# Decay exponents of the state-space block as one fp32r product with a block-diagonal matrix kept in DRAM

## The reference, cut to what matters

```python
def _ssd(xs, dt, a, bm, cm):            # 2 chunks of L = 128 tokens, 32 heads
    a_dt = (dt * a)...                   # [chunk, head, 128]
    a_cs = jnp.cumsum(a_dt, axis=-1)
    seg = a_cs[..., :, None] - a_cs[..., None, :]
    decay_in = jnp.exp(jnp.where(tril, seg, -jnp.inf))
    cb = jnp.einsum('bclgn,bcsgn->bgcls', Cc, Bc)
    y_diag = jnp.einsum('bgecls,bcsgep->bclgep', cb[:, :, None] * decay_in, X)
    ...
```

## Time and profile before

| | |
|---|---|
| median of 3 runs | 2217.0 us (2216.79 to 2220.03) |
| profiled execution | 2215.97 us, span 2214.2 us |
| granted TensorE clock | 0.995 of full speed over the span |
| TensorE busy | 2175.9 us, 98% of the span |
| VectorE, ScalarE, GpSimd busy | 1422.0, 999.5, 102.6 us |
| DMA | 409.23 MB, mean 185 GB/s |

### The profile page before, as it was taken

One profiled execution on the slowest core, in us unless ns is written; L12 is line 12 of the kernel. 1 busy time (PEld: TensorE's weight loads), 2 busy tenths in 40 slices (PEclk: granted clock), 3 DMA queues, 4 the chain that ended last, 5 costly groups with the idle time before them and its releaser, 6 DMA issues.

```text
span 2214.2 us, 29921 instructions
## 1 busy us (share of the span) xinstructions
PE 2175.9 (98%) x11250; PEld 1794.6 (81%) x11250; DVE 1422.0 (64%) x2126; ACT 999.5 (45%) x1486; POOL 102.6 (5%) x122
## 2 busy tenths in 40 slices
PE   6999999999999999999999999999999999999999
PEld 1587888897778888888778888888888888888887
DVE  2267665646846676787788545687778787644455
ACT  3243242434544444555466445544444444344453
POOL 1020100102010120000000000000000000000000
PEclk8999999999999999999999999999999999999999
DMA  9976565543045666665413565666666666655674
GB/s 372 384 227 209 200 209 187 164 122 97 10 167 177 211 200 190 180 184 174 148 39 94 181 190 185 211 191 183 192 180 189 187 189 190 200 190 190 190 244 164
DMA packets 209908, 409.23 MB, mean 185 GB/s; under 512 B 15501, under 2 KB 24069, under 8 KB 208264
## 3 DMA queue, kind: packets, MB, share of 16 engines
q1 hardware_dynamic: 205536, 386.71, 55.7%
q0 software_dynamic: 3360, 16.76, 2.6%
q10 hardware_dynamic: 904, 4.29, 0.5%
HBM read 400.49 MB, written 7.22 MB: 184 GB/s over the span
## 4 chain that ended last, share of the span: by engine, by line
PE 90%; DVE 4%; DMA 3%; ACT 1%; issue 1%; POOL 0%; SPq 0%; DVEq 0%; ACTq 0%
PE bank L2085 52%; PE bank L2095 19%; PE bank L2099 10%; DMA ada_ring<-in_w_ada 2%; PE bank L2211 1%; PE bank L2321 1%; PE bank L2269 1%; PE bank L2308 1%; DVE wlo L1283 1%; PE bank L2235 1%; PE bank L2220 1%; DMA raw<-in_w_in 1%; PE bank L2499 0%; DVE st L1489 0%; PE bank L2391 0%
## 5 line engine op out<-in xcount | busy, mean ns | idle before, releaser
L2085 PE MATMUL bank<-whi,xhl 128*128 128x512 f32 (+2 forms) x3776 | 1136.7, 383 | 3.4 <-DVE wlo L1283 3.0
L1283 DVE TENSOR_TENSOR wlo<-raw,whi 128x1024 fp32r<-128x1024 f32 (+2 forms) x649 | 773.2, 1204 | 463.7 <-ACT whi L773 442.4
L773 ACT ACTIVATE whi<-raw 128x1024 fp32r<-128x1024 f32 (+2 forms) x649 | 664.1, 1047 | 667.1 <-PE bank L2085 344.6
L2085 PEld LDWEIGHTS bank<-whi,xhl 128*128 128x128 f32 x3776 | 695.5, 188 | 140.1 <-DVE wlo L1283 6.5
L2085 PE MATMUL bank<-wlo,xhl 128*128 128x512 f32 (+2 forms) x1888 | 719.9, 381 | 0.0
L2095 PE MATMUL bank<-xhl,whi 128*128 128x512 f32 x1792 | 489.4, 394 | 0.0
L2085 PEld LDWEIGHTS bank<-wlo,xhl 128*128 128x128 f32 x1888 | 354.4, 188 | 67.4
L2095 PEld LDWEIGHTS bank<-xhl,whi 128*128 128x128 f32 x1792 | 306.3, 189 | 41.5 <-issue 0.3
L2099 PEld LDWEIGHTS bank<-xhl,wlo 128*128 128x128 f32 x1792 | 275.0, 189 | 38.2
L2099 PE MATMUL bank<-xhl,wlo 128*128 128x256 f32 x1792 | 285.0, 281 | 0.0
L1946 DVE TENSOR_TENSOR up_x<-bank,up_x 128x256 f32<-128x256 f32 x88 | 31.2, 417 | 72.2 <-ACT up_x L780 72.2
(11 more groups left out here) (361 smaller groups left out, 1383.8 us busy)
## 6 DMA issues: line engine op xcount, KB each, us to landing
raw<-in_w_in SPq DMA_DIRECT2D x216, 512.0 KB, 4.1
raw<-in_w_up SPq DMA_DIRECT2D x176, 512.0 KB, 3.7
raw<-in_w_out SPq DMA_DIRECT2D x96, 512.0 KB, 4.6
raw<-in_w_down SPq DMA_DIRECT2D x88, 512.0 KB, 4.7
ada_ring<-in_w_ada SPq DMA_DIRECT2D x64, 512.0 KB, 11.4
gate_w<-in_w_ada SPq DMA_DIRECT2D x32, 512.0 KB, 3.9
raw<-in_w_ple_gate SPq DMA_DIRECT2D x32, 512.0 KB, 4.8
raw<-in_w_in SPq DMA_DIRECT2D x16, 384.0 KB, 3.8
```

The costliest lines, as they stand in the source:

```text
L773: nc.scalar.activation(whi[:, slot, 0:size], raw[:, slot, 0:size], ACT.Copy).then_inc(hi_ready, 1)
L1283: tt_(wlo[:, slot, 0:size], raw[:, slot, 0:size], whi[:, slot, 0:size].bitcast(F32), ALU.subtract).then_inc(lo_ready, 1)
L2085: ins = mm(b4[tt][:, 0:width], x[:, o:o + P], w, start=k == 0 and i == 0, stop=k == last and i == 2)
```

## The change

It builds the exponents another way. The cumulative sums themselves are computed by TensorE with heads on partitions (one 128x128 product for each chunk, from a copy of a_dt that stands four times side by side, the last two times negated), and are split into a high and a low fp32r part (`CH`, `CL`).

- A DRAM tensor `m_dram` of 2 x 128 x 4096 floats holds, for each head, a block of 128 columns. It is first filled from the constants, which grow by 4096 columns (two copies from DRAM to DRAM of 2 MB each, on GpSimd's queue, right behind the load of `h` and ahead of the constants). Later four DMAs write the positive high and low sums on its block diagonal, rows 0 to 63. Rows 64 to 127 keep ones in each head's block.
- `STA`, the stationary operand of a chunk, has ones in rows 0 to 63 and the negated high and low sums in rows 64 to 127. One fp32r product of `STA` with 512 columns of `m_dram` then gives sum at l minus sum at s for four heads.
- The mask is added in the same bank by an fp32r product of the identity with the mask (0 or -1e30), read four times.
- `RR` is no longer computed: GpSimd loads 256 KB of `m_dram` into it for each batch, so `seg_rows` is gone from VectorE and ScalarE.
- In the loop over b the batches of `seg` are now issued in pairs, behind the products of odd b.

```diff
...
+K_DIAG = 1610
+K_W = K_DIAG + 4096
...
+    c[:, K_SLT:K_SLT + P] = np.where(i[:, None] <= i[None, :], 0, NEG)
+    for h in range(32):
+        c[64 + h::32, K_DIAG + P * h:K_DIAG + P * (h + 1)] = 1.0
...
+        m_dram = nc.dram_tensor("cumsum_diag_dram", (NT, P, 4096), F32).ap()
...
             g.dma_start(H[:, :, :], a["x"][0].rearrange("(t p) n -> p t n", p=P)).then_inc(s_h, 16)
+            for t in range(NT):
+                g.dma_start(m_dram[t], a["const"][:, K_DIAG:K_DIAG + 4096]).then_inc(s_mz, 16)
             g.dma_start(KC2[:, :], a["const"][:, K_SWA:K_SWA + 5 * P]).then_inc(s_t5, 16)
...
+            g.wait_ge(s_mz, 32)
+            g.wait_ge(s_clo, 1)
+            for t in range(NT):
+                for rows, part in ((0, CH), (32, CL)):
+                    corner = m_dram[t, rows:rows + 1, 0:1]
+                    diag = bass.AP(corner.tensor, corner.offset, [[4096 + P, 32], [1, P]])
+                    g.dma_start(diag, part[rows:rows + 32, t, :].bitcast(F32)).then_inc(s_md, 16)
+            g.wait_ge(s_md, 64)
+            g.wait_ge(xb_ready, 6)
+            for b in range(16):
+                if b == 2:
+                    g.wait_ge(xd_ready, 1)
+                if b >= 4:
+                    g.wait_ge(seg_ps, b - 3)
+                g.dma_start(RR[b % 4][:, :, :].rearrange("p h l -> p (h l)").bitcast(F32),
+                            m_dram[b // 8, :, W * (b % 8):W * (b % 8 + 1)]).then_inc(seg_in[b % 4], 16)
...
+                if i == 4:
+                    act.wait_ge(s_cst, 1)
+                    copy(CH[:, :, :], bank[3][:, 0:2 * P].rearrange("p (t l) -> p t l", t=NT)).then_inc(s_chi, 1)
+                if i == 7:
+                    act.wait_ge(s_clo, 1)
+                    copy(STA[0:64, 0, :], KC2[0:64, 512:640])
+                    own(copy(STA[0:64, 1, :], KC2[0:64, 512:640]))
+                    copy(STA[64:96, :, :], CH[64:96, :, :].bitcast(F32))
+                    copy(STA[96:128, :, :], CL[96:128, :, :].bitcast(F32))
+                    copy(MSKR[:, :], KC2[:, 384:512])
+                    copy(IDR2[:, :], ID[:, :]).then_inc(s_sta, 1)
...
+                    for t in range(NT):
+                        for k in range(4):
+                            ins = ts_(ADT4[:, t, 32 * k:32 * k + 32], ADT[:, t, :], 1.0 - 2.0 * (k // 2), None, ALU.mult)
+                    ins.then_inc(s_adt4, 1)
...
+                if i == 5:
+                    dve.wait_ge(s_chi, 1)
+                    tt_(CL[:, :, :], bank[3][:, 0:2 * P].rearrange("p (t l) -> p t l", t=NT),
+                        CH[:, :, :].bitcast(F32), ALU.subtract).then_inc(s_clo, 1)
...
-                tt_(RR[b % 4][:, :, :], tri3, b32(ADT[:, t, h0:h0 + 4], P), ALU.mult).then_inc(seg_in, 1)
...
             def seg(b):
...
+                pe.wait_ge(seg_in[b % 4], 16 * (b // 4 + 1))
                 if b >= 4:
                     pe.wait_ge(seg_e, b - 3)
-                mm(bank[b % 4][:, :], SLT, RR[b % 4][:, :, :].rearrange("p h l -> p (h l)"), start=True,
+                mm(bank[b % 4][:, :].rearrange("p (h l) -> p h l", h=4), IDR2[:, :],
+                   MSKR[:, :].rearrange("p (h l) -> p h l", h=1).to_broadcast([P, 4, P]), start=True, stop=False)
+                mm(bank[b % 4][:, :], STA[:, b // 8, :], RR[b % 4][:, :, :].rearrange("p h l -> p (h l)"), start=False,
                    stop=True).then_inc(seg_ps, 1)
...
+                    pe.wait_ge(s_adt4, 1)
+                    for t in range(NT):
+                        ins = mm(bank[3][:, P * t:P + P * t], ADT4[:, t, :], TRI, start=True, stop=True)
+                    ins.then_inc(s_cst, 1)
...
-                if b + 4 < 16:
+                if b % 2 and b < 13:
+                    seg(b + 3)
                     seg(b + 4)
...
```

More of the change, by code:

```diff
@@ L194, in build @@
         MR = [at(f"m_ring{i}", o, [P, 4, P]) for i, o in enumerate((51032, 51544, 8192))]
-        RR = [at(f"r_ring{i}", o, [P, 4, P]) for i, o in enumerate((47104, 47616, 43008, 43520))]
+        RR = [at(f"r_ring{i}", o, [P, 4, P], FR) for i, o in enumerate((47104, 47616, 43008, 43520))]
+        ADT4, STA = at("adt_signed", 50656, [P, NT, P]), at("cumsum_stationary", 50656, [P, NT, P], FR)
+        CH, CL = at("cumsum_high", 51032, [P, NT, P], FR), at("cumsum_low", 51288, [P, NT, P], FR)
+        MSKR, IDR2 = at("decay_mask_r", 50384, [P, P], FR), at("ident_r2", 50512, [P, P], FR)
         BT = at("b_t", 48128, [P, 4, P])
@@ L297, in build @@
         yo_ps, yo_done = sem("y_off_psum"), sem("y_off_added")
-        seg_in_a = sem("seg_in_by_scalar")
-        seg_in, seg_ps, seg_e, m_ready = sem("seg_in"), sem("seg_psum"), sem("seg_exp"), sem("m_ready")
+        seg_in = [sem(f"seg_rows_loaded{i}") for i in range(4)]
+        seg_ps, seg_e, m_ready = sem("seg_psum"), sem("seg_exp"), sem("m_ready")
+        s_adt4, s_cst, s_chi, s_clo, s_sta = (sem("adt_signed"), sem("cumsum_rows_psum"), sem("cumsum_high"),
+                                              sem("cumsum_low"), sem("cumsum_stationary"))
+        s_mz, s_md = sem("cumsum_diag_zeros"), sem("cumsum_diag_stored")
         y_mm, y_out = sem("y_products"), sem("y_added")
@@ L1123, in _ @@
             act.wait_ge(qk_ready, 1)
[L1124 to L1131, removed]
             for b in range(16):
@@ L1713, in dt_part @@
                     own(stt(DT, DT_V, 0.0, DT_L, ALU.max, ALU.add))
-                    stt(ADT, DT, -1.0, DT_EA.rearrange("p (a h) -> p a h", a=1).to_broadcast([P, NT, 32]),
-                        ALU.mult, ALU.mult).then_inc(s_dt_v, 1)
+                    own(stt(ADT, DT, -1.0, DT_EA.rearrange("p (a h) -> p a h", a=1).to_broadcast([P, NT, 32]),
+                            ALU.mult, ALU.mult))
+                    dve.sem_inc(s_dt_v, 1)
+                    for t in range(NT):
+                        for k in range(4):
+                            ins = ts_(ADT4[:, t, 32 * k:32 * k + 32], ADT[:, t, :], 1.0 - 2.0 * (k // 2), None, ALU.mult)
+                    ins.then_inc(s_adt4, 1)
                     own(ts_(NSINK, S2[:, 96:128], -1.0, None, ALU.mult))
@@ L1874, in _ @@
                 tt_(m_ring(b), m_ring(b), over_heads(CBT[:, t, g4, :], 4), ALU.mult).then_inc(m_ready, 1)
-                if b + 4 < 16 and b + 4 not in SEG_BY_ACT:
-                    seg_rows(b + 4)
                 if b == 3:
@@ L2380, in _ @@
             jobs(N_O1, J_O1, O1_T, 256, moving=R_O1)
-            TRI, SLT, ONE = KC2[:, 256:384], KC2[:, 384:512], KC2[:, 512:640]
+            TRI, ONE = KC2[:, 256:384], KC2[:, 512:640]
             def seg(b):
[L2384 to L2388, removed]
+                pe.wait_ge(seg_in[b % 4], 16 * (b // 4 + 1))
                 if b >= 4:
                     pe.wait_ge(seg_e, b - 3)
-                mm(bank[b % 4][:, :], SLT, RR[b % 4][:, :, :].rearrange("p h l -> p (h l)"), start=True,
+                mm(bank[b % 4][:, :].rearrange("p (h l) -> p h l", h=4), IDR2[:, :],
+                   MSKR[:, :].rearrange("p (h l) -> p h l", h=1).to_broadcast([P, 4, P]), start=True, stop=False)
+                mm(bank[b % 4][:, :], STA[:, b // 8, :], RR[b % 4][:, :, :].rearrange("p h l -> p (h l)"), start=False,
                    stop=True).then_inc(seg_ps, 1)
```

16 lines of the change are left out of this document (2 added, 14 removed).

## The result

| | before | changed |
|---|---|---|
| median | 2217.01 us (6 runs, 2216.78 to 2220.03) | 2225.97 us (6 runs, 2225.2 to 2228.47) |
| profiled execution | 2215.97 us, span 2214.2 | 2226.18 us, span 2224.4 |
| granted TensorE clock over the span | 0.995 | 0.992 |

The ratio is 1.004, with a 95% interval of 1.0029 to 1.005: the change costs 9.0 us. The forecast was 2225.8 us.

What follows compares the result with a forecast made beforehand. TensorE, busy 98% of the span, was taken as the bound. Profiled execution 2215.97 - 5.6 (loop) + 14.4 (fill) = 2224.8 us; the median, 1.0 us above, gives 2225.8 us; 8-in-10 range 2212 to 2234.

Steps and rivals of the forecast that it cites:

- The fill's loss: Start of the first output projection: the fill of m_dram starves the weight stream, TensorE loses 14.4 us; chance 0.52.
- the length of the fill: Two DRAM-to-DRAM copies behind the load of h: 22.1 us, with reading and writing sharing 403 GB/s.
- the margin: Near 650 us: VectorE has tiles A and B ready 3.5 and 3.6 us before TensorE comes to them.
- The loop's side: Loop of decays, 1093 to 1134 us: 6.2 us less, 0.6 us added on TensorE, so 5.6 us gained.
- Packets one to one: During the fill, DMA engines alternate queues packet by packet whatever the size; weights get about 256 packets of 2 KB, 0.52 MB.
- The case of no starving: Rival at the fill: the weight queue gets what it asks for, TensorE never waits; 2211.4 us, chance 0.19.
- the third case: The fill hardly hurts the weights, for instance if engines drain many descriptors per turn; 2211.4 us, chance 0.19.
- the short case: At the fill: each byte counts once at 403 GB/s, so it lasts 11.7 us and the loss is 4.0 us.
- The small copies "at nothing": Eight small copies and one subtraction on VectorE (some 1.5 us), ScalarE's copies (some 2 us): no cost, covered by ScalarE's waits.
- the lower bound of 3 us: Loop of decays: gain of only 3 us if VectorE and ScalarE hold the pace from batch 5 on.
- that rival: Loop of decays: RR loads need 12 us and come late, 13.5 us on top, 2239 us; chance 0.03.
- The rival of a short fill: At the fill: a byte counts once, over in 11.7 us, loss 4.0 us; 2215.4 us, chance 0.26.

Runs made afterwards that it cites:

- e7: The kernel before with TensorE's part alone: exponents' product in fp32r, seg_rows kept, no fill, cumulative sums or loads; 2219.56 us against 2217.65, ratio 1.0008.

## Why the prediction was right, and where it was not

The time came out within 0.2 us of the forecast. That is closer than the steps deserve, and the closeness is luck. The fill's loss was to be 14.4 us and was 13.7, but the length of the fill and the margin behind this sum were each wrong by several microseconds, in opposite directions. The loop's side was to be -5.6 us and was -3.4 (-4.7 + 0.9 + 0.45). For the profiled execution the sum gave 2224.8 us and 2226.18 came; the 1.0 us added for the median, which lay 0.2 us below that execution this time, made up for it.

**Packets one to one: right.** 318 against 319 in the fill, and 616 against 616 when both had 2 KB. The run with small rows shows that this is what starves the weights. The case of no starving falls with it. The Trainium skill ("DMA: Bandwidth & Descriptors", queues, rings and completion order) has an engine drain a packet of some 9 to 17 descriptors before it changes rings. The change packet by packet agrees with this trace, 318 against 319. The many descriptors in a turn, on which the third case leaned, are not seen here: a turn was one record of the profile, 2 KB of weights against 16 KB of the fill.

**The length of the fill: too long.** I took 22.1 us, from the assumption that reading and writing share the 403 GB/s of the earlier trace rows. It was 14.2 us, between the short case (11.7) and the long one and nearer to the short: 4.15 MB in 14.2 us are 292 GB/s with each byte counted once, beside 0.62 MB of weights. Read and written, that is 584 GB/s, so the two sides don't share 403. The weights did not slow it either. In the run with early copies no weights were loaded beside them, and from 519.6 to 533.4 us the fill moved 4.10 MB, which is 297 GB/s:

```profile
q0 software_dynamic: 285, 4.10, 88.8%
```

The Trainium skill ("DMA: Bandwidth & Descriptors", latency and other measured facts) gives 207 to 214 GB/s for such copies between tensors whose rows lie far apart (512 KiB, or 4 MiB and a little); this trace, with rows 22.8 KB apart where they are read and 16 KB where they are written, has more. Tile A was there for ScalarE at 652.46, not 655.1, and B at 660.53, not 666.5.

**The margin: the step that failed.** "The margin is 3.5 and 3.6 us" compared the end of VectorE's low part of a tile with TensorE's start on that tile. But TensorE's next tile needs a second thing of VectorE, the activations' low half `xhl`, and this stands in VectorE's list *behind* the low part of a weight tile that TensorE wants later. In the kernel before, the record that follows tile A's low part in VectorE's timeline is:

```profile
648.12 0.68 DVE L1329 TENSOR_TENSOR xhl<-bank,xhl 128x512 fp32r<-128x512 f32 x1
```

and TensorE's:

```profile
648.73 0.39 PE L2085 MATMUL bank<-wlo,xhl 128*128 128x512 f32 x1
648.96 0.62 PE L2085 MATMUL bank<-whi,xhl 128*128 128x512 f32 x2
```

`xhl` is done at 648.12 + 0.68 = 648.80, TensorE starts at 648.96. The margin was 0.16 us. So every microsecond by which tile A was late counted: A came 652.46 - 645.89 = 6.6 us later, and TensorE waited 6.43 us. TensorE's two waits together were 9.0 us. A trace without any fill shows the same edge: in the kernel with TensorE's part alone, whose program is the same up to this place, the loads happen to come later, and TensorE waits:

```profile
649.61 0.73 PE L2089 MATMUL bank<-whi,xhl 128*128 128x512 f32 x2 [0.31 <-DVE xhl L1333]
...
653.24 0.73 PE L2089 MATMUL bank<-whi,xhl 128*128 128x512 f32 x2 [0.62 <-DVE xhl L1333]
```

**The clock: missing.** All 14.4 us were to be waiting. In the trace 9.0 us are, and the rest of the 13.7, about 4.7 us, is TensorE working at half clock behind them: it is busy for 5.5 us of the first stretch at half level and for 3.4 of the second, 8.9 us of which full clock would have saved about half. A shorter fill, no margin and a slow clock made 13.7; a long fill, a false margin and full clock made 14.4.

**The small copies "at nothing": wrong by 0.9 us.** I had covered them by ScalarE's slack between 1000 and 1085 us, but the eight copies on VectorE stand near 781 us, where VectorE runs close ahead of TensorE. Moving them to GpSimd takes the step away. ScalarE's copies cost nothing that shows. The products of cumulative sums cost 0.45 us, the distance to the next record, for the 0.6 forecast; their four records:

```profile
1013.09 0.69 PE L2443 MATMUL bank<-const,adt_signed 128*128 128x128 f32 x4
1013.54 0.70 PE L2107 MATMUL bank<-whi,xhl 128*128 128x512 f32 x2
```

**The loop: right in kind, large by 1 to 1.5 us.** The head gave 3.43 - 1.87 = 1.56 us, as forecast (1.6). All of it gave 4.7 us here and 5.2 us in a trace without half clock, for 6.2. In the traces with 13.6 us at half level it gave only 0.6 and 0.4, below the lower bound of 3 us, and the bound knew no clock. The part of it that belongs to `seg_rows` on VectorE and ScalarE is no side matter: with TensorE's part alone the kernel gains nothing. I had given 4 of 6.2 us to TensorE's shorter product; by e7 a shorter product pays nothing without the removal of `seg_rows`. The removal alone wasn't tried, so how much of the gain it brings by itself stays open. The loads of `RR` were never late, so that rival falls too.

**The sum:** +13.7 + 0.9 + 0.45 - 4.7, less the 0.2 us by which it was ahead at 629 us, is 10.1 us, the shift at the end; the spans differ by 10.2. The rival of a short fill named 2215.4 us; it had the length nearly right and fails on the margin.

## What to carry to other kernels

A DMA of large rows on a second queue takes turns with a weight stream packet by packet, so count packets, not bytes: put such a transfer where the stream rests, which here turned +9.0 us into -3.4 by the medians (-0.4 to -4.7 by the ratio's interval), or cut it into rows as small as the stream's. To read a margin, list everything that the waiting instruction needs, and take the one that stands furthest back in its producer's list. And when TensorE is given less to do while others hold the pace, look at the granted clock as well as at the waits, in more than one execution.

## What was unexpected of the hardware

- TensorE's granted clock went to its half level in an idle stretch of 6.4 us (near 650 us), but also in the loop, in e7 during the second of two waits of 1.14 and 1.92 us, and stayed there for 3.4 to 13.6 us at a time; behind it the same eight products took 1.97 us for 1.00. Waits alike in other executions (1.3 us in the kernel before and with early fills) had no such fall behind them.
- With 10 us less work on TensorE the kernel was not faster (1.0008, 0.9998 to 1.0017), and 3.7 us of useless work put back on top did not make it slower (1.0001).
- A copy from DRAM to DRAM in rows of 16 KB ran at 292 GB/s beside the weight stream and at 297 alone, each byte counted once.
- The DMA engines took the two queues' packets in turn, whatever their size (318 against 319, 616 against 616), so the queue with packets of 16 KB got 4.15 MB and the one with 2 KB got 0.62.
